# Modulation rows of the second layer: four items moved from TensorE in the gated-delta heads to VectorE in the attention pairs

## Chip, cores and metric

One Trainium2 chip, one NeuronCore of it. The metric is the device time of one execution of the whole program in microseconds, from the first to the last instruction and what lies around them; lower is better. All data is float32 in HBM.

## What is computed

Two layers over 512 tokens of 1024 features. Each has a token mixer (layer 0: gated DeltaNet with 8 heads of 128; layer 1: forgetting attention with 16 heads of 64) and a mixture of 32 experts of which each token takes 2. Ahead of the layers, a conditioning vector `c` gives each layer six rows of 1024 numbers (shift, scale and gate of both sublayers):

```python
c_act = jax.nn.silu(c)
for i in range(DEPTH):                       # DEPTH = 2
    ada = (c_act @ ada_w[i] + ada_b[i])[:, None, :]      # 1024 x 6144 weights a layer
    sh1, sc1, g1, sh2, sc2, g2 = jnp.split(ada, 6, axis=-1)
    h = rms_norm(x) * (1.0 + sc1) + sh1
    y = gdn_mixer(h, ...) if i % 2 == 0 else fox_mixer(h, ...)
    x = x + g1 * y
    h = rms_norm(x) * (1.0 + sc2) + sh2
    x = x + g2 * hier_moe(h, ...)
return rms_norm(x, final_norm)
```

The attention of layer 1, for each head and each tile of 128 queries: scores against all earlier keys, plus a bias from the cumulated forget gates, softmax, product with v; then a gate `sigmoid(g_out)`.

## The kernel before

**Items and parts.** The twelve rows of 1024 numbers are twelve *items*, numbered layer * 6 + (shift 1, scale 1, gate 1, shift 2, scale 2, gate 2). The weights of an item are 4 MB, cut into four quarters of 1 MB (two blocks of 128 inputs by 1024 outputs each). A *part* is one quarter: `quarters` (L741 to L752) issues 8 matmuls, which use `cact` (the activated vector, one column per block) as weights, repeated over 32 columns, and stream 256 columns of `Dr` each; four strips of the array make four column ranges of the item. Four parts make an item; VectorE adds the bias (`ada_item`, L1832 ff.), ScalarE stores the row to DRAM (`ada_rows`).

**Where they run.** Items 0 and 1 come first of all. The ten others run in the gated-delta heads: `ADA_HEADS = 5`, eight parts a head in heads 0 to 3, four parts in head 4 and the last four in head 7. In a head, `one_corrected` on TensorE is a loop over six levels of a triangular inverse; between the steps of a level it puts pieces of the next head's projection (`fill`) and the parts (`ada_parts`). SyncE loads the quarters into the two halves of `Dr` when they come free.

**The attention pairs.** The 16 heads of layer 1 are worked in 8 pairs, pair 0 and pair 7 by themselves and the others in a loop. For each pair, four engines run in step over four query tiles, of width 128, 256, 384 and 512:
- TensorE (`attend`, L1246 ff.): scores (L1269), transposes of the normalized softmax tiles (L1285), products with v (L1295). Between them it puts the projection of the next pair (`fill`, 96 matmuls L771 to L773 a pair). In the last pair these are replaced by 28 matmuls of the output projection (L994).
- VectorE (`attend`, L2289 ff.): adds the bias and takes the maximum (L2303), negates it (L2306), then the reciprocal of the sum (L2310) and the normalization (L2311) of both heads; behind the third and the fourth tile the low part of a square for the next pair (L2287, `square_low`); at the end 1/(1+e) of the gate (L2315, L2316) and the gated output (L2319).
- ScalarE: the exponentials (L1645), evictions (L1335) and the high part of the weights of the pair after the next (L1335, `Whi`).
- GpSimd: the causal bias tiles of the pair (L2561) and the low part of those weights (L2385, `Wlo = Wr - Whi`). Its last such work for a pair is in pair 5.

All engines take their instructions in program order and wait on semaphores.

**SyncE's queue in layer 1.** `pair_load` (2 MB of projection weights for the pair after the next, when the projection of the next one is done), `bias_rows` (512 KB of gate sums for the next pair). ScalarE waits for the weights ahead of the first exponential of a pair. Behind the loop: the two halves of the output weights, X, the weights of experts 0 and 4 (`after_projection`), then `sublayer_rows(1)`: `modq` (shift 2 and scale 2 by features, read by TensorE's L1022 ahead of the output projection), `gateB`, and more. `load` (L447) is the helper that issues all loads, so all of them carry its line.

## Time and profile before

| | us |
|---|---|
| three timed runs | 1476.53, 1471.62, 1475.49 (median 1475.49) |
| profiled execution, whole | 1471.81 |
| its span, first to last instruction | 1470.2 |
| TensorE (PE) busy in the span | 1340.3 (91%) |
| VectorE (DVE) | 730.6 (50%) |
| ScalarE (ACT) | 436.1 (30%) |
| GpSimd (POOL) | 397.3 (27%) |
| mean granted clock of TensorE | 0.966 of full |

The stages by the start of their projections: gated-delta heads from about 72 to 472, output projection and routing to 545, experts of layer 0 to 800, attention pairs from 857 to 1116, output projection and routing of layer 1 to 1193, experts to 1441. A row of the trace names the engine, the line of the kernel, the operation and `out<-in` with the tile names (`PS` is PSUM, `arena` a large block of SBUF in which most small tiles lie). Busy time counts instructions in flight; a wait is the idle time ahead of an instruction with the one that ended it. In the rows below, "pair 4" is the inner pair whose TensorE work starts at about 990.4.

### The profile page before, as it was taken

The page shows a single profiled execution, that of the slowest core. Times are in us where ns is not written, and L with a number is a line of the kernel's source. Part 1 is how long each engine was busy: PE and PEld are TensorE (multiplying, and loading weights), DVE is VectorE, ACT ScalarE, POOL GpSimd, SP SyncE. Part 2 cuts the span into 40 slices and gives each one's busy share as a digit, 9 for nine tenths or more (in the row PEclk, how much of TensorE's full clock was granted, in tenths as well). Part 3 has the DMA queues.
Part 4 walks back from the last instruction along what each step waited for, and adds up shares of the span by engine and source line. Part 5 has one row for each costly group of instructions (what it writes and reads, how often), then busy time and mean ns, then how long its engine had stood idle before and what let it go on. Part 6 is the DMA issues. An engine that isn't in the chain of part 4 may idle for free.

```text
span 1470.2 us, 24718 instructions
## 1 busy us (share of the span) xinstructions
PE 1340.3 (91%) x8999; PEld 868.3 (59%) x8999; DVE 730.6 (50%) x1513; ACT 436.1 (30%) x1033; POOL 397.3 (27%) x588
## 2 busy tenths in 40 slices
PE   3999999999998989999786999999999979999881
PEld 2677777777775455555342777777764544555440
DVE  3756566657552466522223545666654557322224
ACT  4434424444442110000002655555541200000002
POOL 3022012202230022444234054434410024434320
PEclk9999999999999989999998899999999999999996
DMA  8265555412154369999998221122056379999995
GB/s 356 117 227 199 206 205 197 174 63 108 58 220 126 124 251 395 417 418 421 421 420 321 97 87 73 72 78 107 28 190 240 154 281 417 420 419 418 419 390 194
DMA packets 56693, 350.27 MB, mean 238 GB/s; under 512 B 18408, under 2 KB 18880, under 8 KB 30992
## 3 DMA queue, kind: packets, MB, share of 16 engines
q1 hardware_dynamic: 44992, 332.02, 56.9%
q0 software_dynamic: 11520, 16.83, 3.1%
q8 instruction: 68, 1.11, 0.3%
q14 instruction: 33, 0.27, 0.1%
q10 hardware_dynamic: 80, 0.04, 0.0%
HBM read 342.45 MB, written 27.34 MB: 252 GB/s over the span
## 4 chain that ended last, share of the span: by engine, by line
PE 69%; DMA 15%; DVE 11%; ACT 2%; issue 2%; SPq 0%; POOL 0%; DVEq 0%; POOLq 0%; ACTq 0%
PE PS L1091 10%; DMA hT<-in_moe_w_down_dram 8%; PE PS L771 7%; PE PS L773 7%; PE PS L772 6%; PE PS L1034 6%; PE PS L1098 5%; DMA Dr<-in_ada_w_dram 4%; PE PS L749 2%; PE PS L869 2%; PE PS L1118 2%; PE PS L1108 2%; PE PS L884 2%; PE PS L1083 2%; PE PS L1269 2%
## 5 line engine op out<-in xcount | busy, mean ns | idle before, releaser
L771 PE MATMUL PS<-hHi,Whi 128*128 128x512 f32 x512 | 224.5, 439 | 2.7 <-DVE hLo L1762 2.4
L773 PE MATMUL PS<-hHi,Wlo 128*128 128x512 f32 x512 | 202.4, 395 | 0.0
L772 PE MATMUL PS<-hLo,Whi 128*128 128x512 f32 x512 | 201.4, 393 | 0.0
L1335 ACT COPY arena<-PS 128x512 f32<-128x512 f32 (+3 forms) x256 | 110.1, 446 | 284.2 <-PE PS L869 116.4
L1091 PE MATMUL PS<-Wr,arena 128*64 128x256 f32 x1408 | 166.9, 391 | 9.8 <-DVE arena L2162 9.8
L1556 ACT ACTIVATE arena<-PS 128x128 f32<-128x128 f32 x72 | 20.0, 278 | 467.4 <-PE PS L1091 386.5
L1091 PEld LDWEIGHTS PS<-Wr,arena 128*64 128x64 f32 x1408 | 102.2, 141 | 89.4 <-issue 30.2
L2444 POOL DMA_INDIRECT y_rows<-arena x72 | 76.8, 1067 | 258.7 <-DVE arena L2174 253.0
L2385 POOL TENSOR_TENSOR Wlo<-Wr,Whi (+1 forms) x72 | 93.9, 1323 | 178.3 <-ACT Whi L1335 178.3
L771 PEld LDWEIGHTS PS<-hHi,Whi 128*128 128x128 f32 x512 | 97.2, 190 | 34.2 <-issue 19.3
L2168 DVE TENSOR_TENSOR arena<-arena,PS 128x128 f32<-128x128 f32 x72 | 20.7, 288 | 185.4 <-ACT arena L1556 185.2
L773 PEld LDWEIGHTS PS<-hHi,Wlo 128*128 128x128 f32 x512 | 96.8, 189 | 22.3
L2174 DVE TENSOR_TENSOR arena<-PS,gateB 128x512 f32<-128x512 f32 x72 | 49.7, 691 | 114.6 <-PE PS L1098 60.6
L772 PEld LDWEIGHTS PS<-hLo,Whi 128*128 128x128 f32 x512 | 97.6, 191 | 13.8 <-issue 1.4
L2439 POOL DMA_INDIRECT arena<-h_rows,arena x72 | 75.9, 1055 | 97.5 <-DVE arena L2152 42.7
L2412 POOL TENSOR_TENSOR arena<-arena,negmask 128x512 f32<-128x512 f32 x48 | 74.0, 1576 | 65.4 <-DVE arena L1856 65.4
L1034 PE MATMUL PS<-Wr,arena 128*128 128x512 f32 x200 | 87.7, 595 | 3.1 <-DVE X L1962 1.9
L1335 ACT CAST Whi<-Wr 128x512 fp32r<-128x512 f32 x128 | 76.1, 627 | 4.0 <-DMA Wr<-in_fox_w_dram 3.2
L1034 PEld LDWEIGHTS PS<-Wr,arena 128*128 128x128 f32 x200 | 37.4, 190 | 48.9 <-issue 44.0
L1881 DVE TENSOR_TENSOR arena<-arena,PS 128x256 f32<-128x256 f32 (+1 forms) x48 | 20.1, 419 | 89.8 <-PE PS L884 65.5
L2162 DVE COPY arena<-PS 128x512 f32<-128x512 f32 x72 | 49.7, 691 | 18.8 <-PE PS L1083 14.8
L2396 POOL COPY taps<-cols 128x12 f32<-128x12 f32 x8 | 1.6, 198 | 210.1 <-DVE arena L1818 210.1
(387 smaller groups left out, 2330.5 us busy)
## 6 DMA issues: line engine op xcount, KB each, us to landing
Wr<-in_moe_w_gate_up_dram SPq DMA_DIRECT2D x52, 2048.0 KB, 17.3
Dr<-in_ada_w_dram SPq DMA_DIRECT2D x42, 1024.0 KB, 27.2
Dr<-in_moe_w_down_dram SPq DMA_DIRECT2D x28, 1024.0 KB
arena<-in_moe_w_gate_up_dram SPq DMA_DIRECT2D x14, 2048.0 KB, 20.0
hT<-in_moe_w_down_dram SPq DMA_DIRECT2D x26, 1024.0 KB
Wr<-in_gdn_w_dram SPq DMA_DIRECT2D x8, 2048.0 KB, 8.5
Wr<-in_fox_w_dram SPq DMA_DIRECT2D x8, 2048.0 KB, 7.9
shift_scale<-in_moe_w_down_dram SPq DMA_DIRECT2D x12, 1024.0 KB
```

What stands on the lines that cost most here:

```text
L771: mm(out_ap, a_hi, b_hi, start=(k == 0), stop=False)
L772: mm(out_ap, a_hi, b_lo, start=False, stop=False)
L773: return mm(out_ap, a_lo, b_hi, start=False, stop=(k == KD - 1))
L1034: last = mm(PS[u % 2][:], tile(OT[:, k, :], n), Wr[:, nh, k, :], start=(k == 0), stop=(k == KD - 1))
L1091: last = mm(out_bank[C * g:C * g + C, 0:DE], at, w[:, k, g * DE:g * DE + DE], start=(k == 0), stop=(k == KD - 1))
L1098: last = mm(out_bank[C * g:C * g + C, :], act_t[:, C * k:C * k + C], w[:, k * D + g * 512:k * D + g * 512 + 512], start=(k == 0), stop=(k ...
L1335: return nc.scalar.copy(dst, src)
L2162: cpv(xgT[u].rearrange("p k j -> p (k j)"), PS[2 + u][:]).then_inc(m["xt"], 1)
L2385: g.tensor_tensor(Wlo[:, at, :], Wr[:, 0:2].rearrange("p s k n -> p (s k) n")[:, at, :], Whi[:, at, :], ALU.subtract).then_inc(w_lo_pool, 1)
L2412: g.tensor_tensor(t4(nt[l]), t4(aT), negmask[:, l:l + 1, :].to_broadcast([P, NT, P]), ALU.mult).then_inc(nt_ok, 1)
L2439: g.indirect_dma_start(out=xg[u], out_offset=None, in_=rows_of, in_offset=bass.IndirectOffsetOnAxis(ap=rows, axis=0), bounds_check=2 * T - ...
L2444: g.indirect_dma_start(out=y_rows[i], out_offset=bass.IndirectOffsetOnAxis(ap=sidx[:, at, :], axis=0), in_=yo[u], in_offset=None, bounds_c ...
```

## The change

`ADA_HEADS` goes from 5 to 3. Items 2 to 7 stay in the gated-delta heads: eight parts in heads 0 and 1, four in head 2, four in head 7. The items 8 to 11 (gate 1, shift 2, scale 2, gate 2 of layer 1) are made on VectorE in the attention pairs, half an item (512 outputs) per pair, eight halves in eight pairs. A quarter is now 512 KB, loaded into one half of the upper row of `Dr`. VectorE multiplies each of the 8 blocks of 128 inputs by its column of `cact` and accumulates over 128 partitions x 512 columns; TensorE then sums over the partitions with a matrix of ones (four matmuls of 32 x 128 outputs), VectorE adds the bias, SyncE stores.

```diff
-ADA_HEADS = 5
+ADA_HEADS = 3
+LATER = 2 + 2 * ADA_HEADS
...
+        later_w = [Dr[:, 1, a * 1024:a * 1024 + 1024].rearrange("p (k c) -> p k c", k=2) for a in range(2)]
+        later_acc = ada_acc[:].rearrange("p i c -> p (i c)")
+        later_made = ada_bias[:, 0, 0:P]
...
+        later_in, later_in_from = (modc_in, cum_out), (32, 16)
+        later_mul, later_sum, later_row = osum_ok, sso_ps, s_ok
...
@@ SyncE
                 if layer == 1:
                     sp.wait_ge(wo_ok, WO)
+                    sp.wait_ge(later_out, 16 * 6 + later_dma_from)
...
+            def later_loads(m, now, then):
+                load(later_made[0:97:32, :], later_half_row(ada_b, *now), later_bias)
+                for q in (2, 3):
+                    sp.wait_ge(later_mul, m * KD + 2 * q - 2 + later_mul_from)
+                    sp.sem_inc(loop_passed, 1)
+                    later_load(*now, q)
+                if then is not None:
+                    for q in range(2):
+                        sp.wait_ge(later_mul, m * KD + 2 * q + 6 + later_mul_from)
+                        sp.sem_inc(loop_passed, 1)
+                        later_load(*then, q)
+            def later_store(m, now):
+                sp.wait_ge(later_row, m + 1 + later_row_from)
+                sp.sem_inc(loop_passed, 1)
+                load(later_half_row(ada_rows, *now), later_made[0:97:32, :], later_out)
+                sp.wait_ge(later_out, m * 16 + 16 + later_dma_from)
+                sp.sem_inc(loop_passed, 1)
...
             bias_rows(0)
+            sp.wait_ge(modc_in, 32)
+            for q in range(2):
+                later_load(LATER, 0, q)
             with sp.Fori(0, 3) as j:
                 for u in range(2):
                     pair_load(j * 2 + (2 + u), u, j * 2 + (1 + u))
                     bias_rows(j * 2 + (1 + u))
+                    now, then = (j + LATER, u), (j + (LATER + u), 1 - u)
+                    later_loads(j * 2 + u, now, then)
+                    later_store(j * 2 + u, now)
             bias_rows(H - 1)
             sp.wait_ge(fpj_ps, 4 * 7)
             out_load(fox_w_out, 0, 0, mix_w[0])
+            later_loads(H - 2, (11, 0), (11, 1))
+            later_store(H - 2, (11, 0))
             after_projection(1)
+            later_loads(H - 1, (11, 1), None)
+            later_store(H - 1, (11, 1))
             sublayer_rows(1)
@@ TensorE, attend
                     fill(*((7, 10), (12, 16), (18, 21), (24, 28))[qt])
+                    if qt == NT - 1:
+                        pe.wait_ge(later_mul, p * KD + KD + later_mul_from)
+                        for j in range(4):
+                            last = mm(PS[7][32 * j:32 * j + 32, 0:P], ones[:, 0:32], later_acc[:, j * P:j * P + P], start=True, stop=True)
+                        last.then_inc(later_sum, 1)
@@ VectorE
+            def later_products(p, k0, k1):
+                for k in range(k0, k1):
+                    if k % 2 == 0:
+                        dve.wait_ge(later_in[k // 2 % 2], p * 32 + (16 * (k // 4 + 1) + later_in_from[k // 2 % 2]))
+                    w = later_w[k // 2 % 2][:, k % 2, :]
+                    if k == 0:
+                        TS(later_acc, w, cact[:, 0:1], None, ALU.mult).then_inc(later_mul, 1)
+                    else:
+                        dve.wait_ge(later_mul, p * KD + k + later_mul_from)
+                        STT(out=later_acc, in0=w, scalar=cact[:, k:k + 1], in1=later_acc, op0=ALU.mult, op1=ALU.add).then_inc(later_mul, 1)
+            def later_item(p):
+                dve.wait_ge(later_sum, p + 1 + later_sum_from)
+                dve.wait_ge(later_bias, p * 16 + 16 + later_dma_from)
+                TT(later_made, PS[7][:, 0:P], later_made, ALU.add).then_inc(later_row, 1)
...
+                    if qt < NT - 1:
+                        later_products(p, (0, 2, 5)[qt], (1, 4, 7)[qt])
                     for a in range(2):
                         u = 2 * qt + a
                         dve.wait_ge(pr_ok, p * 8 + (u + 1))
                         link(nc.vector.reciprocal(rinv[:, u:u + 1], rsum[:, u:u + 1]))
                         TS(pS[a][:, 0:w], pS[a][:, 0:w], rinv[:, u:u + 1], None, ALU.mult).then_inc(pn_ok, 1)
+                    if qt < NT - 1:
+                        later_products(p, (1, 4, 7)[qt], (2, 5, 8)[qt])
                     if more and qt >= 2:
                         square_low(p + 1, qt - 2)
+                later_item(p)
```

The semaphores are old ones of the gated-delta stage that are free by then: in the rows, `osum_ok` counts the products, `sso_ps` the sums, `s_ok` the finished half rows, `ada_out0` their stores, `modc_in` and `cum_out` the loaded quarters.

**TensorE, first level of the head with index 3.** Before:

```order
L869 MATMUL PS<-arena 128x128 x3
L771 MATMUL PS<-hHi,Whi 128x512 [waits ev_pj]
L772 MATMUL PS<-hLo,Whi 128x512
L773 MATMUL PS<-hHi,Wlo 128x512
L749 MATMUL PS<-Dr,cact 32x256 [waits ada_in0]
L749 MATMUL PS<-Dr,cact 32x256 x7
L749 MATMUL PS<-Dr,cact 32x256 [waits ada_in1]
L749 MATMUL PS<-Dr,cact 32x256 x7
L884 MATMUL PS<-arena 128x64 [waits p_ok]
```

With the change (line numbers are those of the changed file):

```order
L926 MATMUL PS<-arena 128x128 x3
L828 MATMUL PS<-hHi,Whi 128x512 [waits ev_pj]
L829 MATMUL PS<-hLo,Whi 128x512
L830 MATMUL PS<-hHi,Wlo 128x512
L941 MATMUL PS<-arena 128x64 [waits p_ok]
```

The two parts between the projection piece and the wait for `p_ok` are gone; the same holds for the other six parts of this head, and for four parts each of the heads with index 2 and 4.

**VectorE, second query tile of an attention pair** (the rows `ISA ... 128x256` are the maximum of L2303 and its read of the accumulator). Before:

```order
L2306 TENSOR_SCALAR arena<-arena 128x1 [waits dve_link]
L2310 RECIPROCAL arena<-arena 128x1 [waits pr_ok]
L2311 TENSOR_SCALAR arena<-arena 128x256 [waits dve_link]
L2310 RECIPROCAL arena<-arena 128x1 [waits pr_ok]
L2311 TENSOR_SCALAR arena<-arena 128x256 [waits dve_link]
L2303 ISA arena<-PS,arena 128x384 [waits sc_ps,pr_ok]
```

With the change:

```order
L2389 TENSOR_SCALAR arena<-arena 128x1 [waits dve_link]
L2364 SCALAR_TENSOR_TENSOR ada_acc<-Dr,cact,ada_acc 128x512 [waits osum_ok,cum_out]
L2364 SCALAR_TENSOR_TENSOR ada_acc<-Dr,cact,ada_acc 128x512 [waits osum_ok]
L2395 RECIPROCAL arena<-arena 128x1 [waits pr_ok]
L2396 TENSOR_SCALAR arena<-arena 128x256 [waits dve_link]
L2395 RECIPROCAL arena<-arena 128x1 [waits pr_ok]
L2396 TENSOR_SCALAR arena<-arena 128x256 [waits dve_link]
L2364 SCALAR_TENSOR_TENSOR ada_acc<-Dr,cact,ada_acc 128x512 [waits osum_ok,modc_in]
L2386 ISA arena<-PS,arena 128x384 [waits sc_ps,pr_ok]
```

Two products stand between the maximum and the reciprocal now, and one, the first to read the third quarter, between the normalization and the next tile's maximum.

**SyncE, around the last two pairs.** Before:

```order
L447 DMA arena<-cum_rows 128x1024 [waits cbt_ok]
L447 DMA Wr<-in_fox_w_out_dram 128x4096 [waits fpj_ps] x2
L447 DMA X<-x_rows 128x4x1024 [waits x_out]
L447 DMA Wr<-in_moe_w_gate_up_dram 128x4096 x2
L447 DMA modq<-ada_rows 128x8x1 [waits wo_ok,ada_out1,ada_out0]
```

With the change:

```order
L458 DMA arena<-cum_rows 128x1024 [waits cbt_ok]
L458 DMA Wr<-in_fox_w_out_dram 128x4096 [waits fpj_ps]
L458 DMA ada_bias<-in_ada_b_dram 4x128
L458 DMA Dr<-in_ada_w_dram 128x2x512 [waits osum_ok] x4
L458 DMA ada_rows<-ada_bias 4x128 [waits s_ok]
L458 DMA Wr<-in_fox_w_out_dram 128x4096 [waits ada_out0,fpj_ps]
L458 DMA X<-x_rows 128x4x1024 [waits x_out]
L458 DMA Wr<-in_moe_w_gate_up_dram 128x4096 x2
L458 DMA ada_bias<-in_ada_b_dram 4x128
L458 DMA Dr<-in_ada_w_dram 128x2x512 [waits osum_ok] x2
L458 DMA ada_rows<-ada_bias 4x128 [waits s_ok]
L458 DMA modq<-ada_rows 128x8x1 [waits ada_out0,wo_ok,ada_out1]
```

The two last quarters of the last half item stand behind four loads of 2 MB, and `modq` stands behind the last half row's store.

## Rows read from the trace of the kernel before

**Rows 1.** Windows of three gated-delta heads, index 3, 4, 5: stretch, us, busy by engine, clock, DMA.

```profile
228.60:280.70 52.10, 51.83 (x394) 39.60 (x394) 31.46 (x61) 21.63 (x48) 9.70 (x8) 1.00 0.56 203
280.70:329.20 48.50, 47.92 (x331) 37.97 (x330) 31.20 (x60) 21.69 (x48) 9.72 (x8) 1.00 0.24 88
329.20:374.80 45.60, 44.19 (x267) 36.24 (x265) 30.72 (x59) 21.64 (x48) 9.67 (x8) 1.00 0.24 93
```

**Rows 2.** The same view of pair 4: PE, PEld, DVE, ACT, POOL busy.

```profile
990.40:1023.80 33.40, 33.23 (x184) 24.17 (x183) 21.70 (x48) 18.72 (x45) 14.66 (x16) 1.00 0.21 78
```

**Rows 3.** Timeline of TensorE in pair 4, transposes: start, us, what, idle before.

```profile
1000.65 0.33 PE L1285 MATMUL PS<-ident,arena 128*128 128x128 f32 x1 [0.17 <-DVE arena L2311]
...
1006.40 0.60 PE L1285 MATMUL PS<-ident,arena 128*128 128x128 f32 x4
...
1012.12 0.82 PE L1285 MATMUL PS<-ident,arena 128*128 128x128 f32 x6
```

**Rows 4.** Timeline of VectorE in pair 4, second and third tile.

```profile
1003.43 0.16 DVE L2310 RECIPROCAL arena<-arena 128x1 f32<-128x1 f32 x1 [0.23 <-ACT arena L1645]
1003.63 1.43 DVE L2311 TENSOR_SCALAR arena<-arena 128x256 f32<-128x256 f32 x1
...
1005.17 1.20 DVE L2311 TENSOR_SCALAR arena<-arena 128x256 f32<-128x256 f32 x1
...
1010.09 0.16 DVE L2310 RECIPROCAL arena<-arena 128x1 f32<-128x1 f32 x1 [0.40 <-ACT arena L1645]
...
1011.34 0.42 DVE L2311 TENSOR_SCALAR arena<-arena 128x384 f32<-128x384 f32 x1
```

**Rows 5.** Timeline of GpSimd in pair 4, low parts of the weights.

```profile
1002.37 3.84 POOL L2385 TENSOR_TENSOR Wlo<-Wr,Whi  x3 [3.58 <-ACT Whi L1335]
1009.73 1.29 POOL L2385 TENSOR_TENSOR Wlo<-Wr,Whi  x1 [3.51 <-ACT Whi L1335]
1011.50 1.40 POOL L2385 TENSOR_TENSOR Wlo<-Wr,Whi  x1 [0.49 <-ACT Whi L1335]
```

**Rows 6.** Single lines over the whole span: ns least/median/most, first and last start.

```profile
L1818 DVE SCALAR_TENSOR_TENSOR arena<-arena,taps x72: 710/751/754, 53.5 to 417.7; 128x512 f32<-128x512 f32 x72
L2287 DVE TENSOR_TENSOR sqr_lo<-arena,sqr_hi x16: 684/1769/1781, 847.0 to 1085.8; 128x512 fp32r<-128x512 f32 x16
```

**Rows 7.** Timelines: SyncE at pair 4 and at the last pair, ScalarE's first exponential.

```profile
990.46 0.33 SPq L447 DMA_DIRECT2D Wr<-in_fox_w_dram  x1
...
1091.33 1.48 SPq L447 DMA_DIRECT2D Wr<-in_moe_w_gate_up_dram  x2
1092.91 14.20 SPq L447 DMA_DIRECT2D modq<-ada_rows  x2
...
998.97 0.40 ACT L1645 ACTIVATE arena<-arena 128x128 f32<-128x128 f32 x1 [2.85 <-DVE arena L2306]
```

**Rows 8.** Landing of modq in the last pair; windows of the whole core there.

```profile
DMA to landing us min/median/max: 20.7/21.2/21.6
...
1110.00:1112.00 2.00, 2.00 (x16) 1.28 (x16) 1.66 (x7) 1.63 (x4) 0.00 (x0) 1.00 0.95 401
1112.00:1114.00 2.00, 2.00 (x12) 1.30 (x11) 1.93 (x4) 0.77 (x2) 0.00 (x0) 1.00 0.65 37
```

**Rows 9.** The page's DMA issues: count, KB each, us to landing.

```profile
Wr<-in_fox_w_dram SPq DMA_DIRECT2D x8, 2048.0 KB, 7.9
...
modc<-ada_rows SPq DMA_DIRECT2D x2, 4.0 KB, 5.1
cum_rows<-arena SPq DMA_DIRECT2D x1, 32.0 KB, 1.6
```

**Rows 10.** Timelines of VectorE and TensorE at the last pair's third tile and its end.

```profile
1104.38 0.56 DVE L2303 CUSTOM_DVE_ANT_0 arena<-PS,arena 128x384 f32<-128x384 f32 x1 [2.12 <-PE PS L1269]
...
1112.49 0.42 DVE L2315 TENSOR_SCALAR arena<-arena 128x512 f32<-128x512 f32 x1
...
1116.31 1.97 PE L1022 MATMUL PS<-routW,modq 128*128 128x36 f32 x16
```

More of the change, by code:

```diff
@@ L670, in bias_rows, with later_load, later_half_row @@
                      cum_rows[ds(p * 2, 2), :].rearrange("a t -> (a t)").partition_broadcast(P), cb_in)
+            def later_load(item, half, q):
+                w = ada_w[item, q] if isinstance(item, int) else ada_w[ds(item, 1), q].rearrange("a p n -> p (a n)")
+                load(later_w[q % 2], w.rearrange("p (k h c) -> p h k c", k=2, h=2)[:, half], later_in[q % 2])
+            def later_half_row(rows, item, half):
+                row = rows[item] if isinstance(item, int) else rows[ds(item, 1)].rearrange("a j c -> (a j) c")
+                return row.rearrange("(h a) (b c) -> h (a b) c", h=2, b=2)[half]
+            def later_loads(m, now, then):
[15 more added lines that the diff above has]
+                sp.sem_inc(loop_passed, 1)
             sp.wait_ge(decay_dve, 7)
@@ L1251, in attend @@
                     pe.wait_ge(sqr_ok, p * 2 + (m + 1))
+                    if m == 0:
+                        if not isinstance(p, int) or p > 0:
+                            pe.wait_ge(later_row, p + later_row_from)
                     mm(bank[:], halves_r[:], sqr_hi[:, m, :], start=True, stop=False)
```

8 lines of the change are left out of this document (added).

## Prediction

> **What bounds the kernel now.** I read the page first, then windows cut at the end of each head's and each pair's projection, then the timeline of one inner pair, then the queue of SyncE around the last pair. TensorE is the bound in both stages that the change touches. In the gated-delta heads it is busy 51.83 of 52.10 us in a head with eight modulation parts, 47.92 of 48.50 with four and 44.19 of 45.60 with none [rows 1]. In an inner attention pair it is busy 33.23 of 33.40 us while VectorE is busy 21.70 [rows 2]. VectorE thus seems to have 11.7 us to spare in a pair, for a load of about 6. That share is an average, however, and the timeline says otherwise where it matters: the transposes of the softmax tiles (L1285) start at 1000.65, 1006.40 and 1012.12 [rows 3], and the VectorE operation that they need (L2311, second of two) ends at 1006.37 in the second query tile (5.17+1.20) and at 1011.76 in the third [rows 4]. In the first tile TensorE already waits 0.17 us for it [rows 3]. So scores, maximum, exponential, normalization and transposes form a chain with 0 to 0.4 us of slack, and the products of the projection between them are just long enough to cover it. Work put on VectorE inside that chain shows in full; work put behind the normalization falls where VectorE waits for the next scores.
>
> **What is removed from the heads.** Sixteen parts leave: four of the head with index 2, all eight of index 3, four of index 4. The windows price this without counting instructions. Index 3 had eight parts and takes 52.10 us, index 4 had four and takes 48.50, index 5 has none and takes 45.60 [rows 1]. Index 2 becomes like index 4 now (-3.6), index 3 like index 5 (-6.5), index 4 like index 5 (-2.9): -13.0 us in all. The loads, the sum on VectorE and the store on ScalarE that go with them lie beside TensorE and are in the windows already. The last four parts stay in the last head. The bounds are -12 and -14, since equal windows differ by 0.1 or 0.2.
>
> **What a pair gains on VectorE.** One tensor_scalar on 128x512 (L2315 is the like: 0.42 [rows 10]), seven scalar_tensor_tensor on 128x512 from SBUF (L1818: 0.75 [rows 6]) and one small sum, about 6 us. By place, in an inner pair:
> - First tile: the 0.42 stands between the maximum and the reciprocal, where VectorE had no idle time. TensorE waits for just this: +0.4. The product behind the normalization is free.
> - Second tile: two products (1.5) before the reciprocal, where VectorE idled 0.23 [rows 4]. GpSimd works here on three low parts of the weights, 3.84 us without a gap from 1002.37 [rows 5]. The two normalizations took 1.43 and 1.20 us [rows 4] and each ends 0.13 to 0.16 us behind the end of one of the three GpSimd operations (1.28 each): VectorE waited for GpSimd's instruction to finish. L2287, which reads two SBUF operands as the new products do, takes 1.77 us at the median of all pairs and 0.68 at best, in a pair where GpSimd is not at the weights [rows 6]. If the new products queue in the same way, the four VectorE operations alternate with the three of GpSimd, and the second normalization ends near 1008.3 on the clock of the pair before (delays of the first tile counted), where 1006.8 was wanted: +1.5. If only the normalizations queue, as they do now, it ends near 1007.3: +0.5.
> - Third tile: again two products (1.5) against 0.40 of idle time [rows 4] and 0.4 of slack; GpSimd has operations at 1009.73 and 1011.50 [rows 5], beside exactly these. Without queueing +0.7, with both products held up +2.3; I take 1.5, between them, since it hangs on who comes first by a tenth of a microsecond.
> - Fourth tile: nothing is added ahead of the normalization. TensorE gets four small matmuls with new weights; the bounds are 0.2 and 0.5, I take 0.35.
>
> That is 3.8 us a pair (bounds 1.8 and 4.7), nearer the upper end since the rows of L2311 and L2287 show the queueing, for the six pairs in which GpSimd makes weights: +22.8 (11 to 28). The seventh has no such GpSimd work, but its third load lies behind 2 MB of output weights: +2.7 (1.5 to 3.5).
>
> The Trainium skill ("SBUF — State Buffer", section "SBUF: two separate sides") says that VectorE and GpSimd share one port pair under an exclusive lock, held for a whole instruction, which VectorE needs in a two-port mode or with two SBUF inputs against a GpSimd operation that reads SBUF. The rows of L2311 and L2287 agree with that; by the rule the third tile would stand at its 2.3, six pairs at 27.6 and the end result at 1506.
>
> SyncE's queue gets, in each pair, a bias, four loads of 512 KB, one store and a wait for that store, and only then issues the next pair's 2 MB of weights. Now these are issued at 990.46, land 7.9 us later and are first waited for by the exponential at 998.97 [rows 7]: 0.6 us of slack. The store can go out when the fourth tile is normalized, and a small store lands in 1.6 us [rows 9], about the time that is left until the next issue. I take no delay, and 0.3 a pair as the other end.
>
> **What the last pair pays.** This is the second large term. Around 1091 SyncE issues four loads of 2 MB (output weights, X, two experts); the last two are in [rows 7]. The transfers keep the DMA engines 95% busy until 1112; after that the rate drops from 401 to 37 GB/s [rows 8]. What is issued behind them lands behind them: modq, issued at 1092.91 and 1093.33, took 20.7 and 21.6 us [rows 8]. After the change the third and fourth quarter of the last half item are issued in this place, from about 1100 on, since the code puts them behind those loads. 512 KB at 410 GB/s are 1.3 us, so the third quarter lands near 1113.3. VectorE waits for it with its fifth product, ahead of the maximum that stood at 1104.38 [rows 10]: 1113.3+0.75 is 9.7 us late. Nothing TensorE has left to do covers it. The two products of the next tile add 1.4, the matmuls 0.3: the pair ends 11.4 later.
>
> Then the modulation rows of the second sublayer (modq, gateB) are asked for only when the last store has landed; until now they were asked for at 1092.91. The last normalization ends where L2315 starts, at 1112.49 [rows 10]; with +11.1 that is 1123.6. Small sum and issue 0.4, store 1.6, issue of the first modq load 0.5, landing 5.1 as for modc, the same form of load with nothing ahead of it [rows 9]: 1131.2 to 1131.8. L1022 reads modq and starts at 1116.31 now [rows 10]. The tail is **15.5 us** later, 11.4 of it from the load and 4.1 from modq. gateB is issued a moment later and needed a few us after L1022: hidden. The experts' first prefetches move along with it.
>
> **The sum.** The profiled execution has 1471.8 (its span 1470.2 and 1.6 around it). 1471.8 - 13.0 + 22.8 + 2.7 + 15.5 = 1499.8. The three timed runs have a median of 1475.5, 3.7 above the profiled one, the lowest of them being as fast as it; for the median I say 1501.
>
> **Rivals.**
> - No queueing with GpSimd: the products cost only their own time, 1.8 a pair. For it: L1818, a scalar_tensor_tensor with two SBUF inputs, never took over 0.754 in 72 instances of the heads [rows 6]. Against it: L2287 and L2311 in the pairs themselves. 12 us less: 1489.
> - The late quarters don't stand behind the 8 MB but share the bandwidth with them. Against it: modq's landing. The last pair pays some 2 instead of 11.4: 1492.
> - Both together: 1480.
> - **Faster**: VectorE's spare 11.7 us take up all products, in the last pair too, and the quarters arrive in time. It decides in the second tile: if the two products end before TensorE's 12 projection products (2.8 us), nothing moves. Left are -13.0, 8 x 0.35 for the matmuls and 4.1 for modq: 1471.8 - 6.1 = 1466, or 1469 beside the median.
> - The heads don't get shorter, since the parts only filled waits: +13, so 1514. The windows of heads without parts speak against it.
>
> **How the numbers follow.** Forecast 0.58, no queueing 0.17, shared bandwidth 0.08, both 0.06, faster 0.06, heads unchanged 0.05. The low end, 1482, lies under the first two rivals; the high end, 1514, takes in the upper bounds of the pairs. A measurement of this kernel can tell about 0.3% (4.4 us) from no change. The case of both lies at the edge of no change (1480 against 1475.5), so same has 0.06, faster 0.06, and the rest is slower, 0.88.
>
> **What the profile after would show.** Heads at index 2, 3, 4 of 48.5, 45.6, 45.6 us. Pairs of 37 us instead of 33.4, with TensorE waiting at the transposes for VectorE's normalization in the second and third tile, and new products of 1.2 us and more where GpSimd is busy. In the last pair VectorE waits some 10 us for a load into Dr, TensorE behind it, and L1022 waits for modq. Pairs that stay under 34 us, or a last pair without a DMA wait, would prove me wrong.

## The result, and the profile after

| us | before | after |
|---|---|---|
| median of the timed runs (4 of each) | 1474.7 (1471.6 to 1476.5) | 1506.5 (1504.7 to 1507.9) |
| ratio, 95% interval | | 1.022 (1.020 to 1.024) |
| span of the profiled execution | 1470.2 | 1506.2 |
| TensorE busy | 1340.3 | 1349.1 |
| VectorE busy | 730.6 | 774.8 |
| mean granted clock of TensorE | 0.966 | 0.954 |

The change makes the kernel 2.2% slower, 31.8 us. The forecast was 1501, range 1482 to 1514. Direction and stages were right; the size was 5.5 us short.

Four differences of start times between the two traces make up the 36.0 us by which the span grew. The first attention pair starts at 844.57 instead of 857.3: **-12.7**. From there to the start of the last pair it takes 260.9 instead of 234.1: **+26.8**. From there to the next load of expert weights, which SyncE issues at the end of the output projection, it takes 64.2 instead of 43.8: **+20.5**. The rest takes 336.5 instead of 335.0: **+1.5**.

**Heads.** Windows of the heads with index 2, 3 and 4: stretch, us, busy of PE, PEld, DVE, ACT and POOL, granted clock, share of the DMA engines, GB/s.

```profile
178.00:226.50 48.50, 47.93 (x331) 37.95 (x330) 31.11 (x60) 21.66 (x48) 9.68 (x8) 1.00 0.24 88
226.50:272.00 45.50, 44.06 (x266) 36.14 (x265) 30.75 (x58) 21.56 (x47) 9.70 (x8) 1.00 0.13 47
272.00:317.90 45.90, 44.46 (x269) 36.53 (x268) 30.97 (x59) 21.93 (x49) 9.70 (x8) 1.00 0.13 47
```

They look like heads with four, none and none of the parts in [rows 1]: 48.5, 45.6 and 45.6 were forecast.

**Pairs.** The same view of pair 3 and pair 4 (counted from 0), cut at the start of their first matmul.

```profile
956.94:994.02 37.08, 34.81 (x191) 24.05 (x189) 27.39 (x57) 19.00 (x45) 15.40 (x16) 1.00 0.37 128
994.02:1032.66 38.64, 36.38 (x191) 24.75 (x189) 27.28 (x57) 19.04 (x45) 15.41 (x16) 0.96 0.35 122
```

Against the 33.40 of [rows 2], a pair takes 37.1, and VectorE is busy 5.7 us more. Pair 4 takes 1.56 more than pair 3 and has the granted clock at 0.96 instead of 1.00. The seven distances between pairs are 36.9, 36.9, 38.6, 37.1, 38.6, 37.1 and 35.8.

The timeline of VectorE in pair 3, second and third tile: start, us, engine, line, operation. L2364 is the product, L2396 the normalization.

```profile
969.12 2.50 DVE L2364 SCALAR_TENSOR_TENSOR ada_acc<-Dr,cact,ada_acc 128x512 f32<-128x512 f32 x2
...
971.73 1.19 DVE L2396 TENSOR_SCALAR arena<-arena 128x256 f32<-128x256 f32 x1
...
973.03 0.35 DVE L2396 TENSOR_SCALAR arena<-arena 128x256 f32<-128x256 f32 x1
...
976.51 3.66 DVE L2364 SCALAR_TENSOR_TENSOR ada_acc<-Dr,cact,ada_acc 128x512 f32<-128x512 f32 x2
```

GpSimd (POOL in the rows) beside it, the low parts of the weights:

```profile
968.07 4.70 POOL L2473 TENSOR_TENSOR Wlo<-Wr,Whi  x3 [3.55 <-ACT Whi L1400]
976.54 1.29 POOL L2473 TENSOR_TENSOR Wlo<-Wr,Whi  x1 [3.77 <-ACT Whi L1400]
978.34 1.28 POOL L2473 TENSOR_TENSOR Wlo<-Wr,Whi  x1 [0.51 <-ACT Whi L1400]
```

And TensorE's transposes (L1350), the third of them with the scores behind it (L1329), of pair 3 and then of pair 4:

```profile
972.98 0.90 PE L1350 MATMUL PS<-ident,arena 128*128 128x128 f32 x4 [0.53 <-DVE arena L2396]
...
980.75 1.07 PE L1350 MATMUL PS<-ident,arena 128*128 128x128 f32 x6 [1.57 <-DVE arena L2396]
981.76 1.13 PE L1329 MATMUL PS<-arena 64*128 64x512 f32 x4
```

```profile
1017.82 1.07 PE L1350 MATMUL PS<-ident,arena 128*128 128x128 f32 x6 [1.56 <-DVE arena L2396]
1018.82 2.02 PE L1329 MATMUL PS<-arena 64*128 64x512 f32 x4
```

Two products alone would take 1.5 us. They take 2.50 in the second tile and 3.66 in the third, where both of them run into one of GpSimd's operations each, and GpSimd is held up in turn (4.70 us for three operations that took 3.84 in [rows 5]). TensorE, which had at most 0.17 us of such a wait in [rows 3], waits 0.5 and 1.6 us for the normalization. Counted from the first matmul of the pair (991.24 for pair 4 of before), the transposes of the second tile start at 16.04 (972.98 less 956.94) instead of 15.16 in [rows 3], those of the third at 23.81 instead of 20.88. The second tile, the first included, thus costs 0.9 and the third 2.05 more.

In pair 4 there is something that no row of before has: the same four score matmuls take 2.02 instead of 1.13 us, right behind the wait of 1.56. For 3.4 us from there the granted clock is at its lower level, 1.2 GHz, and that pair is 1.56 us longer.

**The last pair.** SyncE's queue from its start (1105.47) on:

```profile
1105.41 1.08 SPq L458 DMA_DIRECT2D Wr<-in_moe_w_gate_up_dram  x2
...
1113.49 3.89 SPq L458 DMA_DIRECT2D Dr<-in_ada_w_dram  x2
1142.19 0.58 SPq L458 DMA_DIRECT2D ada_rows<-ada_bias  x1
1144.04 2.09 SPq L458 DMA_DIRECT2D modq<-ada_rows  x2
```

The chain of work that ended last, in the same place: start, us, what.

```profile
1113.49 15.44 DMA Dr<-in_ada_w_dram
...
1142.19 1.63 DMA ada_rows<-ada_bias
1144.04 0.38 SPq L458
1144.47 4.07 DMA modq<-ada_rows
1148.58 3.62 PE PS L1079 x16
```

The product of VectorE that waits for this quarter:

```profile
1128.95 0.75 DVE L2364 SCALAR_TENSOR_TENSOR ada_acc<-Dr,cact,ada_acc 128x512 f32<-128x512 f32 x1 [11.31 <-DMA Dr<-in_ada_w_dram]
```

TensorE's timeline there, and windows across the wait:

```profile
1133.26 1.54 PE L1350 MATMUL PS<-ident,arena 128*128 128x128 f32 x6 [11.78 <-DVE arena L2396]
...
1148.58 3.62 PE L1079 MATMUL PS<-routW,modq 128*128 128x36 f32 x16 [3.07 <-DMA modq<-ada_rows]
```

```profile
1117.50:1123.50 6.00, 3.96 (x20) 1.60 (x18) 0.14 (x1) 0.74 (x2) 0.00 (x0) 1.00 1.00 426
1123.50:1127.00 3.50, 0.00 (x0) 0.00 (x0) 0.00 (x0) 0.00 (x0) 0.00 (x0) 0.68 0.95 392
...
1129.00:1133.00 4.00, 0.00 (x0) 0.00 (x0) 3.75 (x11) 1.42 (x4) 0.00 (x0) 0.50 0.03 11
1133.00:1137.00 4.00, 3.74 (x11) 1.88 (x12) 1.36 (x4) 0.96 (x2) 0.00 (x0) 0.50 0.00 0
```

The quarter of 512 KB is issued at 1113.49 and lands 15.4 us later, when the 8 MB ahead of it are through (426 and 392 GB/s, then 11). VectorE and TensorE stand still for 11.3 and 11.8 us. The clock falls to 0.50 in this wait, 1.2 GHz. It is back at 1.00 from 1138.4 and at 0.50 again when TensorE starts at 1148.58: L1079 takes 3.62 us for what took 1.97 in [rows 10].

### The profile page after: what moved, and what is told of

The parts are those of the page before. It is cut to its first block, busy times and chain, and to the rows that moved or that the text cites. A ratio compares the mean times of both kernels' runs of the same rounds, so it can differ in the third digit from the quotient of the medians.

```text
span 1506.2 us, 24657 instructions
## 1 busy us (share of the span) xinstructions
PE 1349.1 (90%) x8807; PEld 867.5 (58%) x8807; DVE 774.8 (51%) x1581; ACT 438.1 (29%) x1033; POOL 400.4 (27%) x588
## 4 chain that ended last, share of the span: by engine, by line
PE 63%; DMA 15%; DVE 14%; issue 4%; ACT 3%; SPq 0%; POOL 0%; DVEq 0%; POOLq 0%; ACTq 0%
PE PS L1148 10%; DMA hT<-in_moe_w_down_dram 8%; PE PS L1091 6%; PE PS L828 6%; PE PS L830 5%; PE PS L829 5%; PE PS L1155 5%; DMA Dr<-in_ada_w_dram 4%; PE PS L926 2%; PE PS L1175 2%; PE PS L941 2%; PE PS L1165 2%; DVE ada_acc L2364 2%; PE PS L806 2%; PE PS L1329 2%
## 5 line engine op out<-in xcount | busy, mean ns | idle before, releaser
L2473 POOL TENSOR_TENSOR Wlo<-Wr,Whi (+1 forms) x72 | 98.4, 1385 | 198.4 <-ACT Whi L1400 198.3
L828 PEld LDWEIGHTS PS<-hHi,Whi 128*128 128x128 f32 x512 | 98.0, 191 | 35.8 <-issue 20.8
L1091 PE MATMUL PS<-Wr,arena 128*128 128x512 f32 x200 | 91.0, 613 | 1.2 <-DVE arena L1908 1.2
L2364 DVE SCALAR_TENSOR_TENSOR ada_acc<-Dr,cact,ada_acc 128x512 f32<-128x512 f32 x56 | 59.3, 1059 | 15.7 <-DMA Dr<-in_ada_w_dram 14.8
```

Of the source, the lines that this page charges most:

```text
L828: mm(out_ap, a_hi, b_hi, start=(k == 0), stop=False)
L1091: last = mm(PS[u % 2][:], tile(OT[:, k, :], n), Wr[:, nh, k, :], start=(k == 0), stop=(k == KD - 1))
L2364: STT(out=later_acc, in0=w, scalar=cact[:, k:k + 1], in1=later_acc, op0=ALU.mult, op1=ALU.add).then_inc(later_mul, 1)
L2473: g.tensor_tensor(Wlo[:, at, :], Wr[:, 0:2].rearrange("p s k n -> p (s k) n")[:, at, :], Whi[:, at, :], ALU.subtract).then_inc(w_lo_pool, 1)
```

## The experiments

Each was timed beside the kernel before, whose median lay between 1471.5 and 1474.7; the table has the ratio with its interval. The columns in us are read from each profile as above: from the first to the last of the eight pairs (234.1 before), from the last pair to the next load of expert weights (43.8 before).

| kernel | ratio to before | pairs | tail |
|---|---|---|---|
| the changed kernel | 1.022 (1.020 to 1.024) | 260.9 | 64.2 |
| heads_only | 0.994 (0.992 to 0.996) | 234.6 | 43.8 |
| psum_acc | 1.016 (1.012 to 1.019) | 246.8 | 64.5 |
| no_lo | 1.008 (1.005 to 1.010) | 239.3 | 65.1 |
| small_products | 1.027 (1.025 to 1.029) | 245.1 | 61.0 |
| placed | 1.008 (1.005 to 1.010) | 244.0 | 55.7 |
| modq_early | 1.020 (1.016 to 1.023) | 258.1 | 59.4 |
| loads_early | 1.018 (1.015 to 1.020) | 259.2 | 53.7 |
| tail_both | 1.012 (1.009 to 1.016) | 261.0 | 48.7 |
| placed_tail | 0.999 (0.997 to 1.000) | 244.3 | 45.3 |
| placed_tail_psum | 0.994 (0.992 to 0.996) | 238.8 | 45.3 |
| one_sum | 0.995 (0.993 to 0.997) | 238.0 | 45.2 |

### What the heads give

heads_only is the kernel before without items 8 to 11, whose rows are read from items 2 to 5.

```diff
-ADA_HEADS = 5
+ADA_HEADS = 3
...
-                load(gateB[:], ada_row(layer * 6 + 2)[0].partition_broadcast(P), gate_in)
+                load(gateB[:], ada_row(2)[0].partition_broadcast(P), gate_in)
...
```

> The kernel before with ADA_HEADS at 3 and nothing put in place of the parts: items 8 to 11 are left out, and layer 1 reads the rows of items 2 to 5 for them. My theory (TensorE bounds the heads, the parts are on its path): heads with index 2, 3, 4 of 48.5, 45.5 and 45.6 us, the pairs untouched at 33.4, the whole 13 us under the kernel before, 1462. Rival (a wait takes the place of the parts, or the shorter heads collide with something later): less than 8 us of gain, 1467 or more. Since the routing of layer 1 then works on other numbers, the stages up to the last pair are what counts.

The median was 1464.2 against 1473.2, 9.0 us less. The last pair started at 1079.74 instead of 1091.4, 11.7 earlier; the experts behind it, fed with other modulation rows and so routing tokens otherwise, took 338.8 instead of 335.0 us. The heads are worth their 12 to 13 us, and nothing in the pairs eats it (234.6). The rival that they don't get shorter falls. In time it is less than the 13 us that were expected, most of the rest being the 3.8 us of the experts.

### What a product costs beside GpSimd

Three kernels change one side each of the meeting of VectorE and GpSimd. psum_acc keeps the running sum of the products in bank 7 of PSUM, so that a product has one operand in SBUF:

```diff
-                        TS(later_acc, w, cact[:, 0:1], None, ALU.mult).then_inc(later_mul, 1)
+                        TS(PS[7][:], w, cact[:, 0:1], None, ALU.mult).then_inc(later_mul, 1)
...
-                        STT(out=later_acc, in0=w, scalar=cact[:, k:k + 1], in1=later_acc, op0=ALU.mult, op1=ALU.add).then_inc(later_mul, 1)
+                        STT(out=PS[7][:] if k < KD - 1 else later_acc, in0=w, scalar=cact[:, k:k + 1], in1=PS[7][:], op0=ALU.mult, op1=ALU.add).then_inc(later_mul, 1)
```

> The changed kernel with the products accumulated in PSUM bank 7, which is free at that time, so that each product has one SBUF operand and not two; order and number are unchanged. Theory (VectorE's products with two SBUF operands wait for GpSimd's instructions to end): the two products of the second and of the third tile, 2.50 and 3.64 us for two, fall to about 1.5, pairs 0 to 5 get 1 to 2.5 us shorter each, 1494 to 1500 in all. Rival (the products are slow through their dependence on each other, or through memory traffic): same durations, within 2 us of the changed kernel.

no_lo takes the operand away from GpSimd's side: in the pairs it fills with zeros where it subtracted.

```diff
-                    g.tensor_tensor(Wlo[:, at, :], Wr[:, 0:2].rearrange("p s k n -> p (s k) n")[:, at, :], Whi[:, at, :],
-                                    ALU.subtract).then_inc(w_lo_pool, 1)
+                    if low:
+                        g.tensor_tensor(Wlo[:, at, :], Wr[:, 0:2].rearrange("p s k n -> p (s k) n")[:, at, :], Whi[:, at, :],
+                                        ALU.subtract).then_inc(w_lo_pool, 1)
+                    else:
+                        g.memset(Wlo[:, at, :].bitcast(F32), 0.0).then_inc(w_lo_pool, 1)
...
-                    weights_lo(p % 2, p * KD + (H + 2) * KD)
+                    weights_lo(p % 2, p * KD + (H + 2) * KD, low=False)
...
```

> The changed kernel, in which GpSimd's eight subtractions for the low part of the weights in each of the pairs 0 to 5 are replaced by eight fills with zero (so the projections of pairs 2 to 7 lack their low product: the output is not the reference's); the waits and the counts are the same, and GpSimd's loop over pairs 1 to 5 is written out. GpSimd then reads no SBUF beside VectorE's products. Theory (a product is held up by a GpSimd operation that reads SBUF, and holds one up): no product over 0.8 us in these pairs, each tile's cost falls to the products' own time of 1.5 less the idle time they fill, so a pair takes 33.4 + 1.8 = 35.2 instead of 37, and the whole 6 x 1.8 = 11 us less, 1495.5. Rival (a pair's 3.6 us are the products' place ahead of the normalization alone, whatever GpSimd does): 36.5 or more and under 4 us less. Rival (fills hold VectorE up too, since they write through the same port): products of over 1 us beside the fills, and pairs in between, by as much as the fills are shorter than 1.29 us.

small_products shrinks the products to 8 columns, with every wait and load in place.

```diff
-                        TS(later_acc, w, cact[:, 0:1], None, ALU.mult).then_inc(later_mul, 1)
+                        TS(later_acc[:, 0:8], w[:, 0:8], cact[:, 0:1], None, ALU.mult).then_inc(later_mul, 1)
...
-                        STT(out=later_acc, in0=w, scalar=cact[:, k:k + 1], in1=later_acc, op0=ALU.mult, op1=ALU.add).then_inc(later_mul, 1)
+                        STT(out=later_acc[:, 0:8], in0=w[:, 0:8], scalar=cact[:, k:k + 1], in1=later_acc[:, 0:8], op0=ALU.mult, op1=ALU.add).then_inc(later_mul, 1)
```

> The changed kernel with the products on 8 of their 512 columns (the rest of the half rows is left out, the output is not the reference's); all loads, waits, small matmuls and stores stay. Theory (a pair's cost is VectorE's time of the products and what it waits for GpSimd): pairs of 33.7 to 34.0 (33.4 and the small matmuls with their weights), so 3.0 us less in each of six pairs, and the time 1506.5 - 6 x 3.1 - 2 = 1486. The last pair still waits 11 us for the late quarters. Rival (the store's wait on SyncE delays the next pair's weights, or the waits for the quarters cost by themselves): pairs of 35 or more.

The product's line over the whole span, least/median/most in ns; first the changed kernel:

```profile
L2364 DVE SCALAR_TENSOR_TENSOR ada_acc<-Dr,cact,ada_acc x56: 743/752/1876, 854.2 to 1133.7; 128x512 f32<-128x512 f32 x56
```

psum_acc:

```profile
L2364 DVE SCALAR_TENSOR_TENSOR PS<-Dr,cact,PS x48: 744/755/757, 855.2 to 1118.6; 128x512 f32<-128x512 f32 x48
```

no_lo:

```profile
L2364 DVE SCALAR_TENSOR_TENSOR ada_acc<-Dr,cact,ada_acc x56: 743/751/754, 851.2 to 1109.9; 128x512 f32<-128x512 f32 x56
```

small_products:

```profile
L2364 DVE SCALAR_TENSOR_TENSOR ada_acc<-Dr,cact,ada_acc x56: 212/227/1339, 853.9 to 1116.0; 128x8 f32<-128x8 f32 x56
```

In the changed kernel 17 of the 56 products take 1.59 us or more. No product takes over 757 ns once either side has given up its SBUF operand (the eight of psum_acc that write their sum back to SBUF, not shown, take 743 at most). And it is the instruction that waits, not its data: 8 columns take 227 ns alone and up to 1339 where a GpSimd subtraction runs, 1.1 us more, as many as 512 columns do (752 and 1876).

Both kernels confirm the hold-up. Pairs of psum_acc take 35.1, two less than 37.1, and its time of 1495.5 is in the expected range. no_lo gained more than expected: 1482.7 instead of 1495.5 (2.7 us of it lie ahead of the first pair and not in the edit), and its pairs take 34.2, not 35.2. With no product held up, the products and normalizations of second and third tile end before TensorE wants them (its transposes show no wait there), so the time of the products themselves is not paid. Of the 3.7 us of a pair, 2.9 are waiting for GpSimd, that of the normalizations included; the kernel before, with TensorE busy 33.23 of 33.40 us, lost next to nothing to it. The rival that the place ahead of the normalization costs by itself falls. The rival that fills hold VectorE up is half true. Two rows of no_lo, a fill and the normalization that starts beside it:

```profile
998.84 0.53 POOL L2477 MEMSET Wlo<- 128x512 f32 x1 [1.18 <-ACT Whi L1400]
```

```profile
998.92 0.66 DVE L2396 TENSOR_SCALAR arena<-arena 128x384 f32<-128x384 f32 x1
```

The normalization takes 0.66 instead of 0.42, and so in each of the six pairs (0.66 to 0.74); the products beside fills keep 0.75.

small_products was a miss: 34.9 us a pair where 33.7 to 34.0 was expected, and a tenth under the 35 of its rival, by which SyncE's waits cost the time. That rival doesn't explain it, since placed_tail_psum below has the same waits and pairs of 33.9. The theory had put the cost into the length of the products; with products of almost no length a pair still costs 1.5 of the 3.7 us. Some 0.5 to 0.7 of that are the small matmuls (below). The rest fits the meetings that are left: in each of the pairs 0 to 5 two of the eight products still take 1.2 to 1.3 us and one 0.4 to 0.5, instead of 0.23, they put the normalizations behind them off, and TensorE waits 0.5 us for one in the third tile. (Its whole time can't be compared: with rows that lack most products the experts take 359.5 us.)

The Trainium skill ("SBUF — State Buffer", section "SBUF: two separate sides") has these cases as a rule: the shared port pair is taken by a VectorE operation with two SBUF inputs only against a GpSimd operation that reads SBUF, and by a two-port mode against any; "the other fully blocks". The rows above agree, the fill included; which of two operations that start within 0.03 us of each other comes first, they can't show.

### The place of the products

placed moves all but two products of a pair behind the normalizations, into the time when VectorE waits for scores, and the small matmuls behind the transposes of the last tile.

```diff
...
-                    if qt < NT - 1:
-                        later_products(p, (0, 2, 5)[qt], (1, 4, 7)[qt])
+                    if qt == NT - 1:
+                        later_products(p, 5, 7)
...
-                    if qt < NT - 1:
-                        later_products(p, (1, 4, 7)[qt], (2, 5, 8)[qt])
+                    later_products(p, *((0, 2), (2, 4), (4, 5), (7, 8))[qt])
```

> The changed kernel with its eight products at other places of the pair: two behind the normalization of the first tile, two behind that of the second, one behind the third, two between maximum and reciprocal of the fourth (where VectorE waits 2 us for ScalarE), the last behind the fourth normalization; the matmuls with ones stand behind the fourth transposes. Theory (what counts is the place in the chain, not VectorE's total): TensorE's waits at the transposes vanish, inner pairs of 34 us, 16 to 22 us less than the changed kernel, 1485 to 1490. Rival (VectorE's total work and its contention with GpSimd slow the pair wherever the products stand): pairs stay at 36 us or more, under 8 us of gain.

It gave 1483.2, 2 us below the expected range, though its pairs take 35.0 and not the 34 that were expected. The difference is in the last pair, which needs the late quarters later and waits 8.0 us for them instead of 11.3: the tail is 8.5 us shorter. A product is still held up (1.77 us at 1006.32, GpSimd at 1006.15), so place alone does not cure it.

### The tail

modq_early puts the loads of modq, gateB and the rows ahead of the wait for the last half row's store; loads_early puts the weights of experts 0 and 4 behind the late quarters; tail_both does both, with the loads of modq, gateB and the rows ahead of the experts' weights too.

```diff
             after_projection(1)
             later_loads(H - 1, (11, 1), None)
+            sublayer_rows(1)
             later_store(H - 1, (11, 1))
-            sublayer_rows(1)
```

```diff
-                for e in (0, 4)[:2 if layer else 1]:
-                    expert_load(layer, e, e)
+                if layer == 0:
+                    expert_load(0, 0, 0)
...
             later_loads(H - 1, (11, 1), None)
+            for e in (0, 4):
+                expert_load(1, e, e)
             later_store(H - 1, (11, 1))
```

> The changed kernel with one edit on SyncE: modq, gateB and the rows of the second sublayer are asked for ahead of the wait for the last half row's store, as before the change. Nothing else moves: the late quarters still stand behind 8 MB. By the prediction this takes away 4.1 us alone (L1079 no longer waits for modq; 3.07 us of such a wait are in the changed kernel's trace): 1506.5 - 4 = 1502.5, between 1501 and 1504. Rival (the clock was lowered in the last pair by the 11 us wait and stays so whatever stands behind): the same 4 us, no more. Rival (modq's wait was hidden behind ScalarE's or VectorE's own last step): under 1.5 us.

> The changed kernel with the other half of the tail's edit: the weights of experts 0 and 4 (4 MB of the 8 MB) are issued behind the third and fourth quarter of the last half item, but modq still waits for the last store. By the prediction the quarters now have 4 MB (out weights, X) ahead of them, land 10 us earlier, and VectorE's wait for Dr of 11.3 us falls to 0 to 2; modq's 4 us stay. tail_both gave 16.1 in all, so this must give 12: 1494.5, between 1493 and 1497. Rival (the transfers share the bandwidth and the order in the queue does not matter): no more than 2 us. In both kernels the sum of what modq_early and loads_early win should be tail_both's 16; a sum much under it would mean that one wait covers the other.

> The changed kernel with another order in SyncE's queue behind pair 6: output weights, X, the last half item's quarters, then modq, gateB and the other rows, then the weights of experts 0 and 4, then the last store. Theory (the last quarters stand behind 8 MB of transfers, and modq behind the last store): VectorE's wait for a load in the last pair falls from 11.3 to under 3 us, L1079 no longer waits for modq, TensorE's clock stays up there; 15 to 18 us less than the changed kernel, 1489 to 1492. Rival (VectorE's work in the last pair costs the time, or the loads share the bandwidth whatever their order): less than 5 us of gain.

From the last pair to the next expert load it takes 64.2, with modq_early 59.4 (-4.8), with loads_early 53.7 (-10.5), with both 48.7 (-15.5): the two terms add to within 0.2 us. tail_both gave 1490.5, inside its expected 1489 to 1492. In loads_early VectorE waits 1.3 us for Dr and L1079 still 3.1 for modq; in modq_early it is the other way round, 11.7 and none:

```profile
DVE ada_acc L2364 <- DMA Dr<-in_ada_w_dram: 11.7, 1, 11.7
```

(who waits for whom, us in all, times, longest, last pair of modq_early). That the bandwidth is shared, so that the order in the queue doesn't matter, falls with loads_early.

In times, modq_early gave 1499.1 and loads_early 1497.7: 7.4 and 8.8 us below the changed kernel, where 4 and 12 were expected. Set against the kernel before that was timed beside each (1472.6, and 1474.7 for the changed kernel), it is 5.3 and 6.7. Part of this lies in the pairs, and not in the edit: they took 2.8 and 1.7 us less than in the changed kernel. The clock drops of pairs 2 and 4 of the changed kernel fall on pairs 2 and 5 in tail_both, on pair 5 in loads_early and on none in modq_early, though the pairs of all four have the same instructions.

### Together

placed_tail has the edits of placed and tail_both, placed_tail_psum those of psum_acc too.

> The products of a tile stand behind the normalizations (as in placed) and SyncE's order around the last pair is that of tail_both, and the ones matmuls stand behind the transposes of the last tile. Theory (two independent terms): placed measured 1483.2 and tail_both 16.1 us less than the changed kernel; the DMA wait of placed in the last pair was 8.0 us instead of 11.3, so 3 us of those 16 are already gone: 1483.2 - 13 = 1470, between 1466 and 1473, in which pairs stay at 35.0 and the last pair shows no wait for Dr over 2 us. Rival (the terms overlap, since the products now stand later in the last pair and only reach the late quarters when they have landed): only modq's 4 us are won, 1479 or more. Rival 2 (they add in full): 1467.

> As placed_tail, with the products accumulated in PSUM (bank 7), so that only one operand of a product lies in SBUF. Theory that what is left of 1.5 us a pair above 33.4 is still products held up by GpSimd: psum_acc shortened pairs by 1.8 to 3.5 us when the products stood ahead of the normalization, here the most it can give is 1.0 a pair, pairs of 34.0 to 34.3 and 5 to 7 us less than placed_tail. Rival (what is left is the four small matmuls, their weights and their wait on TensorE): pairs stay at 34.8 to 35.1 and the time within 2 us of placed_tail.

placed_tail gave 1471.2 against 1472.6, no difference that can be measured: place and tail together make up for all that the move had cost. placed_tail_psum gave 1465.2, **7.4 us under the kernel before** (0.5% by the medians), with all of the reference's work done, and 6.0 under placed_tail, as expected. The most that this move could give is what heads_only was ahead of the kernel before when the last pair began, 11.7 us (its 9.0 in all are less because of its experts). placed_tail_psum is 8.0 ahead there (1083.4 against 1091.4), and its tail takes 1.5 of them back. Its pairs take 33.9 to 34.1 (the first two 34.4 and 34.6). The same product in the third tile, beside the same GpSimd operation, in placed and then in placed_tail_psum:

```profile
1006.15 1.39 POOL L2472 TENSOR_TENSOR Wlo<-Wr,Whi  x1 [0.49 <-ACT Whi L1400]
1006.32 1.77 DVE L2364 SCALAR_TENSOR_TENSOR ada_acc<-Dr,cact,ada_acc 128x512 f32<-128x512 f32 x1
```

```profile
1001.87 1.39 POOL L2474 TENSOR_TENSOR Wlo<-Wr,Whi  x1 [0.49 <-ACT Whi L1402]
1002.03 0.75 DVE L2366 SCALAR_TENSOR_TENSOR PS<-Dr,cact,PS 128x512 f32<-128x512 f32 x1
```

What is left is 0.5 us a pair. one_sum leaves three of the four small matmuls out.

```diff
-                        for j in range(4):
+                        for j in range(1):
```

> placed_tail_psum with one of the four small matmuls of a pair (three quarters of the half row are left out, the output is not the reference's). Its pairs take 33.9 to 34.1. Theory that what is left above 33.4 is TensorE's own time of the small matmuls and their weights: four matmuls are 0.42 us, three of them 0.3, with what their weight loads cost 0.4: pairs of 33.5 to 33.6 and 3 us less in the whole, 1462. Rival (the first of them pays for a wait or for the change of weights, the others are free): pairs stay within 0.1 of 33.9, 1465.

Pairs stay at 33.9 and the time at 1464.9: the miss is clear. TensorE's timeline at the end of such a pair, first placed_tail_psum (L1352 is the small sum), then one_sum:

```profile
1010.24 1.03 PE L1347 MATMUL PS<-ident,arena 128*128 128x128 f32 x8
1011.20 0.43 PE L1352 MATMUL PS<-ada_acc,ones 128*32 128x128 f32 x8
1011.56 0.50 PE L830 MATMUL PS<-hHi,Whi 128*128 128x512 f32 x1
```

```profile
1010.61 1.03 PE L1347 MATMUL PS<-ident,arena 128*128 128x128 f32 x8
1011.57 0.41 PE L1352 MATMUL PS<-ada_acc,ones 128*32 128x128 f32 x2
1011.90 0.50 PE L830 MATMUL PS<-hHi,Whi 128*128 128x512 f32 x1
```

From the start of the transposes to the next projection matmul it takes 1.32 us with four and 1.29 with one; in pair 4 of before it was 0.8. The interruption costs 0.5 us, and the number of matmuls in it next to nothing. Why one costs that much (its weights, or its wait) was not tried.

## Why the prediction was right, and where it was not

- **Heads, -13.0:** measured -12.7 to the first pair. Right, from the windows alone; the closeness is in part luck, since with the same heads the first pair starts anywhere from 841.8 (no_lo) to 849.3 (placed_tail) in these traces.
- **A pair, +3.8:** measured +3.7 where the clock holds (37.1), and 3.3 in each of the first two pairs. The sum was right and its shares were not. The first two tiles cost 0.9 instead of 0.4 and 1.5; the third 2.05 instead of 1.5; the small matmuls and what follows 0.7 instead of 0.35. In the second tile I let all four VectorE operations alternate with the three of GpSimd, but only two were held, since GpSimd was held up as well. In the third I took the middle between no product held up and both; both were. The forecast had 2.3 for that case, and the row of L2287, held at its median, pointed the same way. (By the rule of the Trainium skill, "SBUF — State Buffer", section "SBUF: two separate sides", the prediction put the third tile at the same 2.3.) Taking the middle of two mechanisms, of which one had the rows behind it, was the weak step. That GpSimd is held up too could be seen in the trace of before: the L2287 at 911.61 starts 0.09 us ahead of a GpSimd subtraction and takes 0.68, and the subtraction takes 1.73.
- **What the 3.8 is made of:** the working gave 1.8 to the products' own time and the small matmuls, and 2.0 to the hold-up. no_lo shows 0.8 and 2.9. The total came out by luck, since the two errors cancel. (With the 0.35 of its own working for the small matmuls the 1.8 would be 1.95; it has 0.2.) That the 1506 which the prediction names by the rule lies at the median is luck too: its six pairs were 27.6 in it (27.3 by its own terms), where the trace has 24.4, the clock's 3.1 included, and the tail made up for it.
- **Clock in the pairs, not priced:** two pairs of 1.6 us more each. With them seven pairs cost 26.8, without them (modq_early) 24.0; forecast 25.5.
- **The seventh pair, 2.7:** measured 2.4 (35.8 against 33.4). VectorE waits 3.5 us for the third quarter (until 1087.84), which stands behind 2 MB of output weights, as forecast.
- **SyncE's wait for the store, 0:** pairs of 33.9 with that wait in place leave little room for it. Right.
- **The last pair, 11.4:** its last products with v start 15.1 us later (1144.42 - 1105.47, against 1115.28 - 1091.40). The mechanism was right, chain, queue and all. It was mis-sized since the quarter landed 23.5 us behind the start of the pair where I had 21.9, and since TensorE came back from its wait at 1.2 GHz: from the third tile's transposes to its products with v it needs 5.3 instead of 3.4 us.
- **modq, 4.1:** TensorE waits 3.1 for it in the changed kernel; without it the tail is 4.8 shorter, which holds the slow L1079 (1.65) that the wait brings about: it takes 3.0 to 3.6 us in the traces in which it waits 2.2 us or more (this one, loads_early, psum_acc, no_lo, small_products) and 1.97 or 1.98 where it waits 1.2 or nothing. L1079 starts 18.2 later, forecast 15.5, and the next expert load 20.5 later.
- **Rivals:** "no queueing with GpSimd" falls with the 1876 ns of L2364. Its argument was L1818 in the heads, which never took over 0.754; but in the head of index 3 of the trace before GpSimd's multiplications end at 243.0, and the first L1818 starts at 250.85, and so it is everywhere: none of the 72 overlaps such a GpSimd operation. The row was quiet since nothing ran beside it, and I had not looked. "Shared bandwidth" falls with the 15.4 us of one 512 KB load, and with loads_early. "Faster" falls as the changed kernel stands. Its idea that VectorE's idle time can take up the products holds once no product is held up and none waits for a load, as placed_tail_psum shows.

The sum had 1499.8, and the profiled execution took 1507.9, the slowest of its four: 8.1 us more (5.5 between the medians). The tail has 5.0 of them, the experts behind it 1.5, the pairs 1.3 and the heads 0.3. TensorE's clock explains the most: 1.65 in L1079, 1.9 in the last pair, 3.1 in pairs 2 and 4, against a size of the pairs that was 1.5 too high without it.

## What to carry to other kernels

Idle time of VectorE beside a busy GpSimd is not free time: an operation with two operands in SBUF can cost the rest of the GpSimd subtraction that it meets, however small it is, so count the meetings and not only the elements, and keep one operand in PSUM. A small load that TensorE's chain needs goes ahead of large prefetches in its queue, and what the next stage reads is asked for before the queue waits for a store. If a wait of several us is brought into TensorE's chain, add what its clock takes afterwards to the wait itself; and an average that leaves 11 us free in a stage says nothing of the chain in it.

## What the runs showed of the hardware

- Two waits of TensorE of 0.5 and 1.6 us in one pair are in some pairs followed by 3.4 us at 1.2 GHz, and in others not: two, two, one and none of the four such pairs (2 to 5) in the changed kernel, tail_both, loads_early and modq_early. Pairs 0 and 1, whose second wait is 1.3 to 1.4 us, never show it, nor does pair 6, with that wait alone. In psum_acc, placed and no_lo, whose transposes wait 0.7 us at most in pairs 0 to 5, no pair shows it. What decides in a single pair stays open; there was no run on it.
- A VectorE operation of 8 columns with two SBUF inputs takes up to 1.34 us when it meets a GpSimd subtraction, and 0.23 otherwise (small_products).
- A GpSimd fill of 128x512 (0.53 us) holds up a tensor_scalar from SBUF to SBUF (0.66 to 0.74 instead of 0.42, no_lo), and not a scalar_tensor_tensor with two SBUF inputs (754 ns at most).
- Four matmuls of 128 columns put between others cost TensorE as much as one of them, 0.5 us (placed_tail_psum and one_sum).
